# Two later starts for the column sums of the second tokens' norms

## The reference, cut to what matters

```python
x = x + mixed @ w_out                      # first block, then its final norm
x = rms_norm(x, final_norm_w)
h = modulate(rms_norm_2(x, norm1_g), sh1, s1)
u = h @ w_pw1 + b_pw1                      # 16 column tiles: pa 0..7 and pg 0..7
u = a * sigmoid(gate)                      # glu
u = silu(layer_norm(dwconv(u, 31 taps)))
x = x + g1 * (u @ w_pw2 + b_pw2)
x = x + g2 * sq_relu_mlp(modulate(rms_norm_2(x, norm2_g), sh2, s2), w1, w2)
```

## Time and profile before

| | us |
|---|---|
| median of 3 runs | 1993.73 |
| lowest, highest | 1992.58, 2003.08 |
| profiled execution, own time | 2001.52 |
| its span, first to last instruction | 1999.7 |
| TensorE busy in it | 1966.9 (98%) |
| mean granted TensorE clock | 0.992 of full speed |

### The profile page before, as it was taken

The page is one execution under the profiler, slowest core; times in us unless marked ns, Lnnn a source line. Parts: engine busy times, 40 slices in busy tenths (PEclk is TensorE's granted clock), DMA queues, the critical chain, the costliest instruction groups (busy, mean ns, idle before and its releaser), DMA issues.

```text
span 1999.7 us, 26668 instructions
## 1 busy us (share of the span) xinstructions
PE 1966.9 (98%) x10026; PEld 1652.0 (83%) x10026; DVE 1256.5 (63%) x2095; ACT 852.9 (43%) x1431; POOL 924.1 (46%) x583
## 2 busy tenths in 40 slices
PE   9999999999999999999999999999999999999997
PEld 7988988988988888888878777777788888888886
DVE  7255455436546365655569988896561845788856
ACT  6433331343543532221445557575643534334321
POOL 3511111112121334343438986686443855877850
PEclk9999999999999999999999999999999999999998
DMA  5301101011021596866435543344457896454432
GB/s 190 106 22 53 51 25 53 32 55 42 22 65 45 179 329 220 271 237 224 127 128 194 184 138 109 119 130 142 143 166 284 305 294 208 136 185 135 142 113 84
DMA packets 94079, 284.38 MB, mean 142 GB/s; under 512 B 10592, under 2 KB 10976, under 8 KB 93824
## 3 DMA queue, kind: packets, MB, share of 16 engines
q1 hardware_dynamic: 70768, 240.20, 35.7%
q10 hardware_dynamic: 23184, 42.48, 6.1%
HBM read 223.39 MB, written 59.24 MB: 141 GB/s over the span
## 4 chain that ended last, share of the span: by engine, by line
PE 86%; DVE 5%; ACT 4%; issue 3%; DMA 1%; POOL 1%; SPq 0%; POOLq 0%; DVEq 0%; ACTq 0%
PE B L1776 43%; PE B L2006 13%; PE B L1955 10%; PE B L1839 7%; PE B L1877 4%; PE B L1904 1%; PE B L1901 1%; PE B L1907 1%; DMA RAW<-wall 1%; DVE HB L2547 1%; PE B L1940 1%; PE B L2081 1%; PE B L1924 1%; PE B L1864 1%; PE B L1916 1%
## 5 line engine op out<-in xcount | busy, mean ns | idle before, releaser
L1776 PE MATMUL B<-HB,WH 128*128 128x512 f32 x2976 | 952.7, 403 | 6.3 <-ACT HB L2206 3.7
L1776 PEld LDWEIGHTS B<-HB,WH 128*128 128x128 f32 x2976 | 549.8, 189 | 130.0 <-issue 18.6
L1776 PE MATMUL B<-HB,WL 128*128 128x512 f32 x1472 | 576.0, 392 | 1.8 <-POOL WL L3122 1.8
L3122 POOL TENSOR_TENSOR WL<-RAW,WH 128x1024 fp32r<-128x1024 f32 x132 | 320.0, 2429 | 349.8 <-ACT WH L2206 348.1
L2206 ACT ACTIVATE WH<-RAW 128x1024 fp32r<-128x1024 f32 (+1 forms) x201 | 204.8, 1024 | 312.9 <-DMA RAW<-wall 292.9
L1776 PEld LDWEIGHTS B<-HB,WL 128*128 128x128 f32 x1472 | 277.7, 189 | 62.2 <-POOL WL L3122 3.1
L3120 POOL TENSOR_TENSOR WL<-RAW,WH 128x512 fp32r<-128x512 f32 x80 | 110.3, 1404 | 309.4 <-ACT WH L2206 309.4
L2547 DVE SCALAR_TENSOR_TENSOR B<-UP,vec,B 128x512 f32<-128x512 f32 x308 | 206.3, 748 | 0.0
L2547 DVE SCALAR_TENSOR_TENSOR RES<-B,modv,RES 128x512 f32<-128x512 f32 x204 | 148.2, 744 | 80.2 <-PE B L2006 57.7
L1839 PE MATMUL B<-WH,HB 128*128 128x256 f32 x768 | 153.2, 297 | 0.0
L3104 POOL TENSOR_TENSOR small<-small 128x4 f32<-128x4 f32 (+2 forms) x36 | 38.5, 1071 | 212.2 <-DVE small L2550 211.8
(11 more groups left out here) (271 smaller groups left out, 3339.4 us busy)
## 6 DMA issues: line engine op xcount, KB each, us to landing
RAW<-wall SPq DMA_DIRECT2D x172, 512.0 KB, 3.8
MODRAW<-wmod ACTq DMA_DIRECT2D x96, 256.0 KB, 5.2
WH<-parts SPq DMA_DIRECT2D x32, 512.0 KB, 3.3
WL<-parts SPq DMA_DIRECT2D x32, 512.0 KB, 4.2
hscr<-HR ACTq DMA_DIRECT2D x64, 256.0 KB, 3.1
HQ<-hscr SPq DMA_DIRECT2D x32, 512.0 KB, 6.4
SUMW<-wall SPq DMA_DIRECT2D x28, 512.0 KB, 7.5
sums<-SUMR SPq DMA_DIRECT2D x25, 512.0 KB, 6.0
```

Source lines behind the costliest of these rows:

```text
L1776: i = pe.matmul(bank, a[:, ks], hb(part, k, h), start=k == 0 and n == 0, stop=k == 7 and n == last)
L3122: i = po.tensor_tensor(lo, raw, hi.bitcast(F32), ALU.subtract)
```

## The change

Two numbers of `make_plan`. `between_blocks(1)` waits 8 steps after the squares instead of 6 before its sums, with `between_blocks(0)` as it was; `before_mlp(1)` waits 2 steps before its sum instead of none, as `before_mlp(0)` did already. What follows in the same generators (the row, `modulated`) moves with them; no instruction is added or removed.

```diff
         held["taps"] = h == 1
-        for _ in range(WAIT[0] + 2 * h):
+        for _ in range(WAIT[0] + 4 * h):
             yield
         add_late()
         take(S, "n1_sum", h)
@@
     def before_mlp(h):
-        for _ in range(0 if h else SUM_LATE):
+        for _ in range(SUM_LATE):
             yield
         add_late()
         take(S, "n3_sum", h)
```

## The result

The changed kernel is slower by a little: its median is 2003.92 us over 14 runs (2000.85 to 2004.48), against 1997.45 us for the kernel before over as many (1992.58 to 2003.08). The ratio is 1.0032, 95% interval 1.0025 to 1.004, some 6.4 us. The three runs that the prediction started from had their median at 1993.73, 3.7 us under that of the fourteen. The profiled execution of after took 2004.2 us, its span 2002.4, the mean granted clock 0.992.

A forecast was written before the change was run, and what follows sets the result against it. TensorE, busy 98% of the span, was taken to set the end by its time without full matmuls at full clock. 1.9 + 2.4 - 0.1 = 4.2 us off the 1993.73 us median gave 1989.5, range 1984.5 to 1998.0.

The forecast's parts named there:

- A: Sums in front of the convolution: 4.40 us lost there, 0.97 of it wait, the rest clock; forecast gain about 1.9 us.
- B: Sum in front of the MLP: moving it gains the whole 2.38 us, 0.68 stall and 1.70 lower clock.
- The order on ACT: First high part stands behind the products of taps 7 and 8, starting at 1046.4 instead of 1046.51.
- the hole: New TensorE idle time of about 2.8 us in front of `pa(3, 0)`, ended by DVE's glu.
- Later on: Engines keep their relative places; later `ysum` at the convolution norm's row costs 0 to 0.2 us, 0.1 in the sum.
- the chain to the glu: DVE takes 9.5 us from first low part to `glu(1, 0)`, which starts 1.87 us earlier.
- the fall in the hole: Clock falls before `pa(3, 0)`, costing 1.70 us, at most 3.4; four in ten, left out; as rival 1991.2, 27%.
- no falls in the median: Median runs had neither clock fall, so B gives its 0.7 us stall and A nothing: 1993.0, 15%.
- The slower rival: First high part waits for tap 8 or 9, over 4 us idle before `pa(3, 0)`, clock falls: 1994.7, 5%.

The follow-up runs named there:

- the kernel with `ysum` kept: The change, with the constant holding `ysum` back 1.7 us smaller, so `ysum(0)` is planned where it stood before: 1998.06 us, ratio 1.0011 to the kernel before.
- MLP-only trace: Kernel before with only the sum in front of the MLP two steps later: median 1995.79 us, ratio 0.9996.
- the kernel before with the early glu: Kernel before with only `glu(1, 0)` planned directly behind its sigmoid, all sums where they stood: 1996.61 us, ratio 0.9999.
- the convolution place alone: Kernel before with only the sums in front of the convolution, and what follows them, two steps later: 2002.16 us, ratio 1.0037.
- the power first: The change, with the split of unit 121 held until `ysum(0)` is written, so POOL takes the norm's power first: 2000.57 us, ratio 1.0021.
- the last experiment: The change, with `glu(1, 0)` directly behind its sigmoid and `ysum` at its place of before, row still later: 1995.91 us, ratio 0.9995.
- taps-behind kernel: The change, with POOL's taps of the first tile held until `modulated("m1", 1)` is written: 2006.97 us, one run.
- the row kept: The change, with two steps fewer between `n1_sum(1)` and `n1_row(1)`, so only the sums are later in the plan: 1995.64 us, ratio 0.9996.
- the early glu on the change: The change, with only `glu(1, 0)` planned directly behind its sigmoid: 1998.47 us, ratio 1.0006 to the kernel before.

## Why the prediction was wrong, step by step

**What held.** The base of the argument, that the sums' waits go and that the clock stays behind them, is in the traces: A's sums at 1034.18 (forecast 1034.27), the row at 1042.14 (1042.26), B without a wait and 2.4 us cheaper than in the earlier trace rows. The order on ACT held to 0.12 us (first high part 1046.28, forecast 1046.4; first low part 1047.03, forecast 1047.15), and the hole stood where it was named, ended by the engine that was named.

**What failed.** The forecast was 4.2 us less, measured are 6.4 more. "Later on" stood in the sum with 0.1 us and costs 4.2. The rest is in the two terms A and B: the kernel with `ysum` kept, which leaves only them, is 2.2 us slower than before where 1.9 + 2.4 were forecast as gained. What is known of that comes in three parts: the baseline, the chain to the glu, and the fall in the hole. Another 3.7 us of the distance from 1989.5 to 2003.92 is the median of only three runs that I subtracted from.

**The baseline.** I took 4.40 us at A, and 2.38 at B, as there to be won in the median. They were those of one execution that had 7.8 us over the median of its three runs and a mean clock of 0.992. Over 73 executions of the kernel before, taken beside the experiments, the clock was 0.996 in 32 (mean 1995.4 us) and 0.992 in two (2002.3). The MLP-only trace (1996.38 us) shows A in an ordinary execution: wait 0.99, no fall, row 8.04 us behind the sums. There the sum of the earlier trace rows is only the wait, and the row, set three k later in the plan, is really later. I had this as the rival "no falls in the median", at 15%, and gave it A worth nothing; by the measured rows it is worth -2.2 us, before the fall in the hole. But the trace of the kernel before with the early glu, 1996.61 us, has the fall at A. So the 3.4 us of clock at A were there in two traces of three, and the 1.7 at B in one of three; B's stall of 0.7 was 0.2 in the other two. The baseline was too high by part of these; by how much in the median no run shows. The sentence of the Trainium skill ("TensorE: Matmul & The Clock Gate", Part 1) on a gate with its own rhythm was the right warning: the wait of 0.97 to 0.99 us with its sixteen small matmuls brought a fall in the earlier trace rows and in the early-glu trace of before, and none in the MLP-only trace.

**The chain to the glu.** I put 9.5 us from the first low part to the glu; it took 10.64. I had read the excess of 1.9 us in the earlier trace rows as waits for high parts. Read singly, the rows of before between those two have no bracket; they have low parts of 1.19, 1.12 and 1.68 us:

```profile
1048.60 1.19 DVE L2547 SCALAR_TENSOR_TENSOR HB<-TM,modv,HB 128x512 fp32r<-128x512 f32 x1
...
1050.37 1.12 DVE L2547 SCALAR_TENSOR_TENSOR HB<-TM,modv,HB 128x512 fp32r<-128x512 f32 x1
...
1052.08 1.68 DVE L2547 SCALAR_TENSOR_TENSOR HB<-TM,modv,HB 128x512 fp32r<-128x512 f32 x1
```

The slow low parts go with POOL's taps, and in after these went on beside three of them (why one of before took 1.68 no run shows); 3 times 0.38 is the missing 1.14. That makes the glu 1.0 us late and the hole 3.79 instead of 2.8.

**The fall in the hole.** I gave it four in ten and left it out. It was there in the traces of the change, of the convolution place alone, of `ysum` kept and of the power first, wherever the hole was 3.79 to 3.81 us, and absent at 1.40. In the change it lasted from 1057.2 to 1064.0, and 1.4 us of that lay in the hole itself: the fourteen matmuls from 1058.56 to 1064.37 took 5.81 us for 3.19, a loss of 2.6 us, where I had 1.70 as its price and nothing in the sum. With `ysum` kept and with the power first it lasted 3.4 us. The mean clock of the change's 14 runs is 0.9931 against 0.9951 of those 73, and among the latter 0.001 of mean clock goes with 1.5 us (a straight line through them), so about 3 of the 6.4 us go with the clock; at a mean clock of 0.993 and 0.994 after still lies 3.9 and 4.7 us above before. What the two profiled executions show for the rest is idle time: 3.5 us more at `pa(3, 0)` and 1.7 at the convolution norm, less 1.0 at A's sums and 0.7 of stall at B, 3.5 in sum.

**Later on.** Here I counted 0 to 0.2 us, and it was 4.2 us between the ratios with and without the later `ysum`. Two things were wrong. The shift was three k and not "some two", by which the 1.38 us in hand were overdrawn (0.57 in the power-first trace). And the step named no queue: of a moved step I followed DVE and TensorE, not POOL, where split 121 stood three k later and takes 2.4 us: by the power-first kernel 2.2 of the 4.2 us go with that queue, the rest with the later place, a split within the error. The later place costs not at this norm alone: in the plan `ysum(1)` moved by three k as well, and a wait of 0.95 to 0.97 us near 1434 stands in all five traces with the later `ysum(0)`, one of 0.22 or 0.23 in the seven others. That DVE and TensorE "stand to each other as before" probably failed as well, by the 2.18 us of the last experiment.

**The slower rival.** It had the right place and mechanism (ACT's queue, a hole near 4 us, the fall), at 5%, but only by the first low part being late; it came to pass with the first low part early, since the chain behind it was longer.

**What stays open.** Whether B gives anything in the median: 0.9996 (0.9984 to 1.0007) holds both nothing and a stall of 0.2 to 0.7. And in which share of executions the clock falls at each place: a profile shows one execution, and only mean clocks are known of the others.

## What to carry to other kernels

A step put later in a list moves everything planned behind it: list each such item with the queue that it passes on every engine, the far ones too, and take off the move (as here, fewer steps of waiting between sums and row) what need not move. Before a clock fall in a profile is counted as a gain, compare that execution's time and mean clock with the other runs, and cost the change on a trace without the fall too. When engines meet at one place, read the instructions singly, since a merged pace hides whether it was waiting or slower work.

## What the runs showed of the hardware

- DVE's low parts (three operands, line 2547, 128x512, written as fp32r) take 0.74 us alone and 1.12 to 1.14 us while POOL adds taps, as after and the taps-behind kernel show side by side (in before and with the row kept single ones took 0.85 to 1.68 beside the taps); the multiplies from PSUM between them stayed at 0.73 to 0.74.
- The clock's falls behind place A, B and the holes lasted 3.4 or 6.8 us (6.8 and 3.4 in before, 6.8 twice in after), and 10.2 once, at the wait of 9.39 us in the taps-behind trace. Where a fall lies partly in idle time it costs less than half its length (2.6 us for 6.8 in after). The same cause did not always bring one: A's wait of 0.97 to 0.99 us did in two traces of three; the 1.94 us of idleness behind the convolution norm's row left the clock at 1.00 in before and in three traces more, and a fall followed it in three others (the MLP place alone among them); 2.5 us at that place brought a fall in after and none in the trace of the early glu on the change.
